# Two norms behind the first network, taken with tokens on partitions

## What is computed

```python
        x = x + g2 * (f @ w_down[l])
    return rms_norm(x, final_norm_g)             # end of first_block
...
    for i in range(DEPTH_2):                     # second_block
        h = _rmsnorm(x, norm_gains[i, 0])
        if i % N_MIXERS == 0:
            h = _rwkv7_time_mix(h, ...)
        x = x + _rmsnorm(h, norm_gains[i, 1])
...
def _rmsnorm(x, g):
    x32 = x.astype(jnp.float32)
    y = x32 * lax.rsqrt(jnp.mean(x32 * x32, axis=-1, keepdims=True) + RMS_EPS)
    return (y * g.astype(jnp.float32)).astype(x.dtype)

def _rwkv7_time_mix(x, mix, w_rkv, w0, w1, w2, ...):
    xx = _token_shift(x) - x
    xs = x[None] + xx[None] * mix[:, None, None, :]
    r, k, v = jnp.einsum('cbtd,cde->cbte', xs[:3], w_rkv)
    xw, xa, xg = xs[3], xs[4], xs[5]
```

## Time and profile before

| | us |
|---|---|
| median of 3 runs | 2099.25 |
| lowest and highest | 2097.47, 2103.8 |
| the profiled execution | 2102.02 |
| its span | 2100.3 |

### The profile page before, as it was taken

The page is one execution under the profiler, slowest core; times in us unless marked ns, Lnnn a source line. Parts: engine busy times, 40 slices in busy tenths (PEclk is TensorE's granted clock), DMA queues, the critical chain, the costliest instruction groups (busy, mean ns, idle before and its releaser), DMA issues.

```text
span 2100.3 us, 35105 instructions
## 1 busy us (share of the span) xinstructions
PE 1981.5 (94%) x14407; PEld 1576.7 (75%) x14407; DVE 1072.7 (51%) x1567; ACT 779.2 (37%) x1241; POOL 256.1 (12%) x282
## 2 busy tenths in 40 slices
PE   7999889999997999899989999999989999999997
PEld 5767668888884677677767788888867877888886
DVE  6776775555325744677643644342254555443323
ACT  4333333333222335667633433322245443233222
POOL 1100000000024000322211211110100021111110
PEclk8999989999999999899988999999989999999998
DMA  8544323333332132000002233333222223333320
GB/s 304 169 125 127 91 61 99 91 100 109 104 89 63 51 93 82 6 10 10 5 27 60 71 95 95 100 109 98 84 60 81 81 80 91 98 92 107 110 83 41
DMA packets 311056, 181.07 MB, mean 86 GB/s; under 512 B 16381, under 2 KB 303763, under 8 KB 310932
## 3 DMA queue, kind: packets, MB, share of 16 engines
q1 hardware_dynamic: 305506, 162.29, 26.1%
q0 software_dynamic: 4608, 16.78, 2.5%
q10 hardware_dynamic: 818, 0.21, 0.0%
HBM read 177.16 MB, written 2.10 MB: 85 GB/s over the span
## 4 chain that ended last, share of the span: by engine, by line
PE 57%; DVE 6%; issue 6%; ACT 2%; POOL 1%; DVEq 0%; POOLq 0%; ACTq 0%
PE bank L258 15%; PE bank L260 14%; PE bank L259 14%; PE bank L2112 4%; DVE x L1308 1%; PE bank L2609 1%; PE bank L1902 1%; PE bank L2603 1%; PE bank L2710 1%; DVE fh_lo L477 1%; ACT fh_hi L473 1%; ACT whi L236 1%; POOL gsq L1569 1%; DVE wlo L243 1%; DVE rstd L370 0%
## 5 line engine op out<-in xcount | busy, mean ns | idle before, releaser
L243 DVE TENSOR_TENSOR wlo<-raw,whi 128x1024 fp32r<-128x1024 f32 (+1 forms) x254 | 331.1, 1304 | 676.7 <-ACT whi L236 676.7
L236 ACT ACTIVATE whi<-raw 128x1024 fp32r<-128x1024 f32 (+1 forms) x254 | 284.1, 1119 | 696.6 <-PE bank L260 689.8
L258 PE MATMUL bank<-fh_hi,whi 128*128 128x512 f32 x992 | 388.1, 391 | 7.1 <-DVE fh_lo L432 6.6
L260 PE MATMUL bank<-fh_hi,wlo 128*128 128x512 f32 x992 | 386.7, 390 | 0.0
L259 PE MATMUL bank<-fh_lo,whi 128*128 128x512 f32 x992 | 386.7, 390 | 0.0
L258 PEld LDWEIGHTS bank<-fh_hi,whi 128*128 128x128 f32 x992 | 186.6, 188 | 49.6 <-DVE fh_lo L432 9.4
L260 PEld LDWEIGHTS bank<-fh_hi,wlo 128*128 128x128 f32 x992 | 186.6, 188 | 39.1
L259 PEld LDWEIGHTS bank<-fh_lo,whi 128*128 128x128 f32 x992 | 186.7, 188 | 38.8 <-issue 0.5
L258 PE MATMUL bank<-f_hi,whi 128*128 128x512 f32 x528 | 205.6, 389 | 0.0
L260 PE MATMUL bank<-f_hi,wlo 128*128 128x512 f32 x528 | 205.4, 389 | 0.0
L259 PE MATMUL bank<-f_lo,whi 128*128 128x512 f32 x528 | 205.4, 389 | 0.0
(11 more groups left out here) (449 smaller groups left out, 3247.4 us busy)
## 6 DMA issues: line engine op xcount, KB each, us to landing
raw<-in_w_up_dram SPq DMA_DIRECT2D x44, 512.0 KB, 3.7
raw<-in_ffn_w_gate_dram SPq DMA_DIRECT2D x44, 512.0 KB, 3.6
raw<-in_ffn_w_up_dram SPq DMA_DIRECT2D x44, 512.0 KB, 3.6
raw<-in_ffn_w_down_dram SPq DMA_DIRECT2D x32, 704.0 KB, 4.4
late<-in_ada_w_dram POOLq DMA_DIRECT2D x32, 512.0 KB, 4.1
raw<-in_rwkv_w_rkv_dram SPq DMA_DIRECT2D x24, 512.0 KB, 4.0
raw<-in_w_down_dram SPq DMA_DIRECT2D x16, 704.0 KB, 4.4
early<-in_ada_w_dram SPq DMA_DIRECT2D x16, 512.0 KB, 14.7
```

What stands on the lines that cost most here:

```text
L236: act.activation(halves_of(at)[0][:, 0:kts * P], raw_unit(at, kts), ACT.Copy).then_inc(hi_ready, 1)
L243: dve.tensor_tensor(lo[:, 0:kts * P], raw_unit(at, kts), hi[:, 0:kts * P].bitcast(F32), ALU.subtract)\
L258: pe.matmul(dst, hi, rhs_hi(k), start=first and k == 0, stop=False)
L260: mm = pe.matmul(dst, lo, rhs_hi(k), start=False, stop=last and k == kts - 1)
```

## The change

It does five things.

1. The class `BothNorms` replaces `Norm` for the first network's last norm. Both sums are taken with tokens on partitions, in eight columns of one bank: plain sums in columns 0 to 3, sums with the gain in 4 to 7.
2. The sums of tiles 0 to 6 (sixteen records) stand in the last unit, ahead of its last three products. Tile 7's sums follow behind the unit.
3. `both_eps`, `both_var`, `both_std`, `both_rstd` are four columns each. PE spreads `both_rstd` over bank 7 and afterwards the first block's `tok_rstd` over bank 6. `hb` and the first block's output read these banks instead of `rstd` in SBUF.
4. ACT squares a tile ahead of the splits of the next tile's units instead of behind them, and a small root (`root_table`) ahead of tile 7's squares makes it load the root's table.
5. The split of unit (0, 1) moves: its upper part on ACT from the network's last pass to behind the two roots, its lower part on DVE from there to behind the first `mix` of the time mix.

The core of the diff:

```diff
+    class BothNorms(Norm):
+        def pe_sums_but_last(self, pe, gsq):
+            wait(pe, std_ready.sem, self.std0)
+            pe.wait_ge(gsq_added, self.n - 2)
+            for t in range(NT):
+                pe.matmul(bank[NORM_BANK][:, NT + t:NT + t + 1], gsq[:, 2, t * P:(t + 1) * P], ones[:, 0:1],
+                          start=t == 0, stop=False, skip_group_check=True)
+            pe.wait_ge(acc_step.sem, self.acc0 + self.n - 2)
+            for t in range(NT):
+                pe.matmul(bank[NORM_BANK][:, t:t + 1], sq_sum[:, t * P:(t + 1) * P], ones[:, 0:1],
+                          start=False, stop=False, skip_group_check=True)
+        def pe_last_sums(self, pe, gsq):
...
+            mm.then_inc(sum_step.sem, 1)
+        def pe_spread(self, pe, dst, columns):
+            for t in range(NT):
+                mm = pe.matmul(bank[dst][:, t * P:(t + 1) * P], columns[:, t:t + 1].to_broadcast([P, P]), ident[:, :],
+                               start=True, stop=True)
+            mm.then_inc(spread_done.sem, 1)
...
-                        if last and q == 1 and g == 1 and not self.conv:
+                        if last and q == 1 and g == 1:
...
+                                if ks[0] == 0 and self.conv:
+                                    self.norm_o.pe_sums_but_last(pe, self.gsq)
...
-            self.norm_o.pe_sums(pe)
-            if self.conv:
-                self.pe_gained_sum(pe)
+            if not self.conv:
+                self.norm_o.pe_sums(pe)
+                return
+            self.norm_o.pe_last_sums(pe, self.gsq)
+            pe.wait_ge(both_step, 3)
+            self.norm_o.pe_spread(pe, SPREAD_BANK, both_rstd)
+            pe.wait_ge(rstd_ready.sem, self.norm_o.rstd0 + 1)
+            self.norm_o.pe_spread(pe, FINAL_BANK, tok_rstd)
...
                         self.norm_o.act_slot_free(act, o - 1)
+                        self.act_gained_square(act, o - 1, 1 - q)
+                        self.norm_o.act_square_of(act, tile_at(x, o - 1), 1 - q)
                     for g in range(2):
                         at = self.at_down(i, 2 * q + g)
                         ends = last and q == 1
-                        if not (ends and (self.final or g == 1 and not self.conv)):
+                        if not (ends and (self.final or g == 1)):
                             split_hi(act, at.plus(2), KD if ends else HALF)
-                    if lagging:
-                        self.act_gained_square(act, o - 1, 1 - q)
-                        self.norm_o.act_square_of(act, tile_at(x, o - 1), 1 - q)
...
-                        if not (ends and self.final):
+                        if not (ends and (self.final or g == 1 and self.conv)):
                             split_lo(dve, at.plus(2), KD if ends else HALF)
...
-        dve.tensor_scalar(tmp[:, 0, :], bank[NORM_BANK][:, :], EPS / D, EPS * EPS, ALU.mult, ALU.add)\
+        dve.tensor_scalar(both_eps, bank[NORM_BANK][:, 0:NT], EPS / D, EPS * EPS, ALU.mult, ALU.add)\
            .then_inc(both_step, 1)
...
-        dve.scalar_tensor_tensor(sq_sum[:, :], bank[GAINED_BANK][:, :], 1.0 / D, tmp[:, 0, :], ALU.mult, ALU.add)\
+        dve.scalar_tensor_tensor(both_var, bank[NORM_BANK][:, NT:2 * NT], 1.0 / D, both_eps, ALU.mult, ALU.add)\
            .then_inc(both_step, 1)
...
-        dve.reciprocal(rstd[:, :], sq_sum[:, :]).then_inc(both_step, 1)
-        dve.wait_ge(both_step, 3)
+        dve.reciprocal(both_rstd, both_std).then_inc(both_step, 1)
+        norm_f.dve_reciprocal(dve)
+        dve.wait_ge(spread_done.sem, norm_f.spread0 + 1)
...
-        act.activation(sq_sum[:, :], sq_sum[:, :], ACT.Sqrt).then_inc(both_std, 1)
+        act.activation(both_std, both_var, ACT.Sqrt).then_inc(both_root, 1)
         norm_f.act_root(act)
+        split_hi(act, at_rkv(0, 1))
...
-            dve.scalar_tensor_tensor(hb[:, k, 1:T + 1], x[:, k, :], gain[:, k:k + 1], rstd[:, :], ALU.mult, ALU.mult)\
+            dve.scalar_tensor_tensor(hb[:, k, 1:T + 1], x[:, k, :], gain[:, k:k + 1], bank[SPREAD_BANK][:, :],
+                                     ALU.mult, ALU.mult)\
                .then_inc(h2_ready, 1)
...
             mix(0, k)
+            if k == 0:
+                split_lo(dve, at_rkv(0, 1))
```

More of the change, by code:

```diff
@@ L414, in dve_rstd, with __init__, act_root, dve_reciprocal @@
             dve.wait_ge(spread_done.sem, self.spread0 + 1)
+    class BothNorms(Norm):
+        def __init__(self, src, n, ready):
+            super().__init__(src, n, ready)
+            self.spread0 = spread_done.claim(2)
+        def pe_sums_but_last(self, pe, gsq):
[9 more added lines that the diff above has]
+        def pe_last_sums(self, pe, gsq):
+            pe.wait_ge(gsq_ready, self.n)
+            for t in range(NT):
+                pe.matmul(bank[NORM_BANK][:, NT + t:NT + t + 1], gsq[:, (self.n - 1) % 2, t * P:(t + 1) * P],
+                          ones[:, 0:1], start=False, stop=True, skip_group_check=True)
+            pe.wait_ge(sq_ready.sem, self.sq0 + self.n)
+            for t in range(NT):
+                mm = pe.matmul(bank[NORM_BANK][:, t:t + 1], sq[:, (self.n - 1) % 2, t * P:(t + 1) * P], ones[:, 0:1],
+                               start=False, stop=True, skip_group_check=True)
+            mm.then_inc(sum_step.sem, 1)
+        def pe_spread(self, pe, dst, columns):
+            for t in range(NT):
+                mm = pe.matmul(bank[dst][:, t * P:(t + 1) * P], columns[:, t:t + 1].to_broadcast([P, P]), ident[:, :],
+                               start=True, stop=True)
+            mm.then_inc(spread_done.sem, 1)
+        def act_root(self, act):
+            act.activation(tok_std, bank[NORM_BANK][:, 0:NT], ACT.Sqrt, bias=eps_col[:, 0:1], scale=1.0 / (self.n * P))\
+               .then_inc(std_ready.sem, 1)
+        def dve_reciprocal(self, dve):
+            dve.wait_ge(std_ready.sem, self.std0 + 1)
+            dve.reciprocal(tok_rstd, tok_std).then_inc(rstd_ready.sem, 1)
     class Split:
@@ L1382, in __init__ @@
                 self.ready = self.o_tile_ready
-                self.norm_o = Norm(lambda k: tile_at(x, k), KD, self.o_tile_ready)
+                self.norm_o = BothNorms(lambda k: tile_at(x, k), KD, self.o_tile_ready)
                 self.out_gate = out_gains
@@ L1457, in down @@
                                               False, True, ready, ks=ks)
-                                if ks[0] == 0:
+                                if ks[0] == 0 and self.conv:
+                                    self.norm_o.pe_sums_but_last(pe, self.gsq)
+                                elif ks[0] == 0:
                                     self.norm_o.pe_sums_but_last(pe)
@@ L1548, in down @@
                 if last and self.conv:
+                    root_table(act)
                     self.o_tile_ready(act, KD - 1)
@@ L1571, in pool_gained_sum @@
                 self.norm_o.pool_add(pool, k)
-        def pe_gained_sum(self, pe):
-            pe.wait_ge(gsq_added, KD - 2)
-            pe.matmul(bank[GAINED_BANK][:, :], ones[:, :], self.gsq[:, 2, :], start=True, stop=False)
-            pe.wait_ge(gsq_ready, KD)
-            pe.matmul(bank[GAINED_BANK][:, :], ones[:, :], self.gsq[:, (KD - 1) % 2, :], start=False, stop=True)\
-              .then_inc(gsq_summed, 1)
         def dve(self, dve):
@@ L1674, in build @@
     gpad_ready = sem("gpad_ready")
-    gsq_ready, gsq_added, gsq_summed = sem("gsq_ready"), sem("gsq_added"), sem("gsq_summed")
-    GAINED_BANK = 5
+    gsq_ready, gsq_added = sem("gsq_ready"), sem("gsq_added")
+    FINAL_BANK = 6
+    both_eps, both_var, both_std, both_rstd = (eps_col[:, n:n + NT] for n in (12, 16, 20, 24))
     w_up0 = A["w_up"].rearrange("a k n -> (a k) n")
@@ L1683, in build @@
     norm_f = ffn0.norm_o
-    both_step, both_std = sem("both_step"), sem("both_std")
+    both_step, both_root = sem("both_step"), sem("both_root")
     x_normed = sem("x_normed")
```

7 lines of the change are left out of this document (3 added, 4 removed).

## The result

| | before | after |
|---|---|---|
| median, 5 runs each | 2098.2 | 2088.13 |
| lowest, highest | 2094.97, 2103.8 | 2084.62, 2092.66 |
| profiled execution, its span | 2102.02, 2100.3 | 2084.62, 2082.8 |

One execution of the kernel before that took 2832.64 us is left out. On one chip the difference is anything from 9.4 (e18) to 14.5 (e1).

What follows compares the result with a forecast made beforehand. It took the chain of waits from the first network's last product to the time mix as the bound. `hb` 6.57 us earlier less 0.41 for the moved split gave 6.2, so 2099.25 - 6.2 gives 2093.1; range 2090.8 to 2096.0.

Steps and rivals of the forecast that it cites:

- Step a: Last unit: two groups of one-column sums cost 0.91 each, delaying the last product by 1.82 us.
- b, c, d: Last product's start to tile 7's `x` 0.49 us; then to first square 0.78; then square 0.72 and hand-over 0.04.
- Step e: Tile 7's sixteen records of sums: 1.05 us for the first eight and 0.91 for the next.
- rival 2: Clock falls before or within the sums; each group of eight loses up to 0.84 us; gain 4.5 to 5.8; chance 0.13.
- f, g: Before the spread: `both_eps` and `both_var`, 2 x 0.20 us; then root's start to spread's start 0.53 and a hand-over.
- Step h: Spread of four columns over a bank before `hb`: 2.00 us at the low clock, plus a hand-over.
- The lower split: Behind the first `mix` on VectorE: takes a 1.14 us slot, less a 0.73 wait that goes; net loss 0.41.
- 1 (the clock stays up): Clock stays at 2.4 GHz through the spread: 0.84 us more, a gain of 7.0, 2092.2; chance 0.25.
- 3 (short ops against masks): VectorE's four short ops meet POOL's masks, 0.39 us each: gain 4.6, 2094.7; chance 0.06.
- 4: Low-rank weights land after TensorE asks at 661.4; a transfer 3 us longer loses 1.1 us, 2094.2; chance 0.02.
- 5 (bank read): Reading the reciprocal root from a bank slows `hb`: 0.4 us over five tiles, 2093.5; chance 0.02.
- 6 (slower, the clock stays down): Clock stays low in the low-rank products: 3.8 us more per tile, 2108.3 with four tiles; chance 0.05.

Runs made afterwards that it cites:

- e18: The changed kernel, unaltered, run again for a third trace: 2091.75, ratio 0.9957 to the kernel before.
- e1: The changed kernel, unaltered, run again for a second trace: 2084.94, ratio 0.9935 to the kernel before.
- e5: The kernel before without the 3.35 us reciprocal, `hb` multiplied by the root itself (values differ): 2096.2, ratio 0.9992.
- e4: The changed kernel with both halves of unit (0, 1)'s split moved, upper behind tile 7's squares, lower behind `gain`: 2089.63, ratio 0.9952 to the kernel before.
- e8: e4 with 17 unused filler products in TensorE's gaps: 2086.81, ratio 0.995 to the kernel before.
- e16: The kernel before with 16 unused one-column products (32 records) in TensorE's gap behind the last wide sum: 2093.88, ratio 0.9976.

## Why the prediction was wrong

**The view of the bound** was right: the path through squares, sums, root and reciprocal decides in that stretch, and e5 gives back the reciprocal's 3.35 in the stretch (3.5).

**Step a** (two groups, 1.82): 1.81 measured. **b, c, d** hold: from the last product's start at 647.91 to `x` 0.44, to the first square 0.78, to the sums 0.77. **Step e** (1.96) is the mis-sized term of the edited place: the first eight took their share (0.92 to the next), the second eight 1.68, since the clock fell at 651, in the middle of them; the sums end 0.64 later than forecast. That is rival 2, in part. **f, g** hold: 0.39 for the two short ops (652.61 to 653.00, forecast 0.40) and 0.47 from the root to the spread (653.00 to 653.47, forecast 0.57). **Step h**: the low clock was right, the first eight records of the spread and the hand-over took 2.12 against 2.04 (653.47 to 655.59). `hb` starts 7.68 after the last product instead of the forecast 7.00, against 15.39.

So 7.71 less 1.81 is 5.90 in place of 6.57.

**The lower split** (net 0.41): from `hb` to the cut at 738.9 the changed kernel takes 0.39 more. The split stands in VectorE's chain (L243, 1.26), the second `hb` starts 5.38 behind the first instead of 4.21, and the wait of the earlier trace rows is gone, as said. But e4, which takes the split out of this chain again, is only 0.2 shorter here. Sum of the edited place: 5.5 for 6.2.

**The rivals.** 1 (the clock stays up) needs the fillers of e8. 3 (short ops against masks) is nil: 0.16 to 0.20 each, and `gain` itself took 0.15 where it had taken 0.55; the section of the Trainium skill's page "SBUF — State Buffer" that the prediction cites against this rival names the 2-port performance modes as a second case, which the prediction's "only" leaves out, and no run here shows that case. 4: the last low-rank load is issued at 649.42 and TensorE starts at 658.03 without a wait for it. 5 (bank read): `hb` takes 0.75 from the bank and took 0.748. 6 (slower, the clock stays down): it is up by 658. 7 is out.

**The step that failed** is the sentence "Every later step and the rest of the program shift with that point". It took the work behind the edit as rigid. It is rigid in what it does, but its instructions stand 40 records further on, and in the blocks, where a product takes a few hundredths of a microsecond, the stops at that place sum to 6.7 us less (11.9 for 18.6), and 32 idle records alone made the kernel before 5.5 us faster. The effect of the edit on TensorE's stream behind it was thus put at nothing without a reason. None of the seven rivals had it, though the stops were in the trace of the kernel before, marked "issue". Had I listed them, the sign could not have been foretold without knowing where they would land, but the range would have had to be some 6 us wider on both sides. That the second part of the gain came out as a gain is luck.

## What to carry to other kernels

An edit that adds or removes instructions on TensorE moves all that stands behind it; where later stages issue many short products, look in the trace for "issue" gaps at even distances in number of instructions, and put their sum into the range. Before crediting a gain to an edit, cut both traces at the same instructions and see in which stage it lies; a kernel with as many added idle instructions helps to tell the edit's own worth (e16 comes near, with 32 of the 40). Here the change's own worth is 5.5 us; the rest is luck of placement, with scatter of the clock on top, and the next edit may take it away again.

## What the runs showed of the hardware

- In a stage of short products, where TensorE gets through 126 or 127 pairs of weight load and product in 4.7 us, it stops at many of the places that far apart, mostly for 0.2 to 1.3 us and in the kernel before once for 2.2; the stops sum to 18.6 us of 342 in these blocks there. It stops where the last packet on the instruction queue started 0.5 to 2.0 us before (242 of 247 places), and goes on 2.1 to 3.0 us after that start.
- With sums of one column between, the clock fell at 651, about 3 us after the last full product, and these sums did not keep it up; the second eight took 1.68 instead of about 1.0.
- Unused work of 2.0 us ahead of `hb` cost 4.7 in total on the means; its trace has more low clock in stages far behind (58.0 us in the blocks), which would explain it but is not shown to.
